# The front of a hybrid decoder block rebuilt: keys projected first, first blocks multiplied chunk by chunk, parts of the preparation moved ahead

## The reference

```python
mod = silu(c) @ w_ada + b_ada
shift1, scale1, gate1, shift2, scale2, gate2 = split(mod, 6)
h = rms_norm(x, norm1_gain) * (1 + scale1) + shift1
proj = h @ w_in
aq, ak, av, dq, dk, dv, dz, dbeta, dalpha, gate_a, gate_b = split(proj)
y_a = sliding_window_attention(rms_norm(aq), rms_norm(ak), av, sinks) @ w_attn_branch
qkv = silu(causal_depthwise_conv([dq, dk, dv]))
g = -exp(dn_a_log) * softplus(dalpha + dn_dt_bias)
od = rms_norm(gated_delta_rule(l2(q), l2(k), v, g, sigmoid(dbeta))) * silu(dz)
y_b = od @ w_dn_branch
mix = (sigmoid(gate_a) * y_a + sigmoid(gate_b) * y_b) @ w_out
x = x + gate1 * mix
h2 = rms_norm(x, norm2_gain) * (1 + scale2) + shift2
x = x + gate2 * peer(h2)      # top-k over 16384 experts, gathers of u and v rows
```

## Time and profile before

| | us |
|---|---|
| median of 3 runs | 2647.77 |
| lowest and highest | 2646.91, 2649.31 |
| the profiled execution, whole | 2649.07 |
| its span, first to last instruction | 2647.2 |
| PE busy in it | 2408.7 |
| DVE busy | 1756.6 |
| ACT busy | 947.5 |
| POOL busy | 734.9 |
| mean granted clock | 0.928 |

### The profile page before, as it was taken

How to read it: one execution, slowest core, us unless ns; L and a number is a source line. 1 busy time by engine, 2 the same in 40 slices (tenths; PEclk the granted TensorE clock), 3 DMA queues, 4 the chain that set the end, 5 groups by cost and what they waited for, 6 DMA issues and landing times.

```text
span 2647.2 us, 34159 instructions
## 1 busy us (share of the span) xinstructions
PE 2408.7 (91%) x13229; PEld 2126.7 (80%) x13229; DVE 1756.6 (66%) x3205; ACT 947.5 (36%) x1628; POOL 734.9 (28%) x661
## 2 busy tenths in 40 slices
PE   8687997878878899988899999989999999999998
PEld 7676776878778778766798999988888888888887
DVE  3468884523425275333398899977888888888887
ACT  1232886020110253222355555543333333333332
POOL 0498500010100000000066653353333333333330
PEclk7798997868869799998999999999999999999999
DMA  6353310000000122321233336689998989899984
GB/s 224 116 155 96 112 49 1 1 1 1 0 0 32 64 87 88 110 98 51 97 124 121 132 128 210 204 306 343 324 318 311 321 314 323 309 328 339 327 312 149
DMA packets 214692, 438.41 MB, mean 166 GB/s; under 512 B 22119, under 2 KB 129808, under 8 KB 214288
## 3 DMA queue, kind: packets, MB, share of 16 engines
q1 hardware_dynamic: 168832, 270.71, 30.4%
q0 software_dynamic: 45568, 163.60, 17.2%
q10 hardware_dynamic: 144, 2.10, 0.2%
HBM read 392.32 MB, written 44.04 MB: 165 GB/s over the span
## 4 chain that ended last, share of the span: by engine, by line
PE 41%; DVE 7%; ACT 1%; issue 1%; DMA 0%; POOL 0%; ACTq 0%; DVEq 0%; POOLq 0%
PE bank L1747 20%; PE bank L1645 5%; DVE hot_j L1963 5%; PE bank L1733 3%; PE bank L1731 3%; PE bank L1732 3%; PE bank L1651 2%; PE bank L1615 2%; DVE hot_i L1958 2%; PE bank L1625 1%; ACT ha L1795 1%; PE bank L1667 1%; DMA vg<-in_peer_v_dram,gidx 0%; DVE o_nat L2027 0%; DVE o_nat L2026 0%
## 5 line engine op out<-in xcount | busy, mean ns | idle before, releaser
L1577 POOL TENSOR_TENSOR ua_lo<-ua,ua_hi 128x512 fp32r<-128x512 f32 x128 | 201.6, 1581 | 576.8 <-ACT ua L1782 576.4
L1747 PE MATMUL bank<-vt_hi,wg_hi 128*128 128x512 f32 x768 | 248.6, 405 | 4.9 <-DVE wg_lo L2017 4.6
L1747 PE MATMUL bank<-vt_lo,wg_hi 128*128 128x512 f32 x768 | 239.1, 393 | 0.0
L1747 PE MATMUL bank<-vt_hi,wg_lo 128*128 128x512 f32 x768 | 238.6, 392 | 0.0
L1570 POOL DMA_INDIRECT ug<-in_peer_u_dram,gidx x128 | 145.6, 1137 | 329.9 <-DVE ug L1973 326.9
L1999 DVE TENSOR_TENSOR vt_lo<-vt_raw,vt_hi 128x1024 fp32r<-128x1024 f32 x128 | 156.2, 1220 | 92.5 <-ACT vt_hi L1869 92.4
L1599 POOL DMA_INDIRECT vg<-in_peer_v_dram,gidx x128 | 131.3, 1026 | 238.2 <-DVE g_acc L1988 226.5
L1645 PE MATMUL bank<-h_hi,ua_hi 128*128 128x384 f32 x512 | 184.2, 360 | 12.3 <-ACT ha L1795 12.0
L1731 PE MATMUL bank<-h_hi,uT_hi 128*128 128x384 f32 x512 | 176.7, 345 | 0.0
L1645 PE MATMUL bank<-h_lo,ua_hi 128*128 128x384 f32 x512 | 174.2, 340 | 0.0
L347 DVE TENSOR_TENSOR mx_lo<-mx_raw,mx_hi 128x2048 fp32r<-128x2048 f32 x32 | 73.2, 2292 | 148.5 <-ACT mx_hi L343 148.5
(11 more groups left out here) (395 smaller groups left out, 5967.9 us busy)
## 6 DMA issues: line engine op xcount, KB each, us to landing
u_raw<-in_peer_u_dram SPq DMA_DIRECT2D x128, 512.0 KB
vt_raw<-in_peer_v_dram SPq DMA_DIRECT2D x128, 512.0 KB
gates<-g_stage SPq DMA_DIRECT2D x12, 2048.0 KB, 8.7
gate<-gates SPq DMA_DIRECT2D x32, 768.0 KB
pj_raw<-in_w_in_dram SPq DMA_DIRECT2D x16, 1024.0 KB, 5.3
ada_w<-in_w_ada_dram POOLq DMA_DIRECT2D x32, 512.0 KB, 4.5
mx_raw<-in_w_in_dram SPq DMA_DIRECT2D x12, 1024.0 KB, 5.2
hid_keep<-ha POOLq DMA_DIRECT2D x64, 192.0 KB, 2.1
```

What stands on the lines that cost most here:

```text
L1577: nc.gpsimd.tensor_tensor(ua_lo[b % 2][:, 4 * q:4 * q + 4, :], ua[b % 2][:, 4 * q:4 * q + 4, :], ua_hi[b % 2][:, 4 * q:4 * q + 4, :].bitca ...
L1747: ins = pe.matmul(y_bank[t][q][:], w[n % 2][:, tok], v[n % 2][:, 512 * q:512 * q + 512], start=(first and i == 0), stop=(last and i == 2))
```

## The change

The condition phase has four buffers for `w_ada`. SP issues slab 0 ahead of x, then the key weights, then slab 2; ACT issues slabs 1 and 3. PE sums slab 0 ahead of x's transposes and the others behind the sums of squares, all in one bank, and DVE adds the bias once. The first two slabs of the projection are now the keys; they are loaded and split within the condition phase, and PE multiplies the first three blocks (`FIRST`) there, a chunk at a time as DVE finishes it. The projection phase starts at block 3. In it `amplitude` comes first on DVE, the key norms' squares behind block 7, the values' low half ahead of the norms' divisions, `decays` ahead of the first convolution. 13 of the 32 sums over `w_ada` stand behind blocks and 19 in the attention steps; POOL fills the masks after chunk 8. The transpose of the running decays moves into the second `mixed`. In the mixing phase slabs 20 and 21, and 24 and 25, are multiplied chunk by chunk in pairs, the second slab three chunks behind (`LAG`), and six of eight mixed chunks are split ahead of slab 21's split.

```diff
-            sp.dma_start(x_nat[:], a["x"].rearrange("o (t p) d -> p (o t) d", p=P)).then_inc(s_x, 16)
...
-            for j in range(ADA_SLABS):
-                if j >= 2:
-                    sp.wait_ge(s_ada, j - 1)
-                sp.dma_start(wada[j % 2][:], wada_v[:, :, 512 * j:512 * j + 512]).then_inc(s_wada[j % 2], 16)
-            sp.wait_ge(s_xt, KC)
+            sp.dma_start(wada[0][:], wada_v[:, :, 0:512]).then_inc(s_wada[0], 16)
+            sp.dma_start(x_nat[:], a["x"].rearrange("o (t p) d -> p (o t) d", p=P)).then_inc(s_x, 16)
             for u in range(2):
-                st.load(sp, 0, u, True, [(slice(0, SLAB), w_in[:, :, SLAB * u:SLAB * u + SLAB])])
+                st.load(sp, 0, u, True, key_pieces(w_in, u))
+            sp.dma_start(wada[2][:], wada_v[:, :, 1024:1536]).then_inc(s_wada[2], 16)
+            for u in range(2):
+                st.load(sp, 1, u, False, [(slice(0, SLAB), w_in[:, :, SLAB * u:SLAB * u + SLAB])])
...
+            def ada(j):
+                pe.wait_ge(s_wada[j], 16)
+                for c in range(4 * j, 4 * j + 4):
+                    for k in range(KC):
+                        last = pe.matmul(bank[7][:, c:c + 1], wada[j][:, k, P * (c % 4):P * (c % 4) + P],
+                                         m.silu_c[:, k:k + 1], start=(k == 0), stop=(k == KC - 1))
+                last.then_inc(s_adac, 1)
+            pe.wait_ge(s_sc, 1)
+            ada(0)
...
-            pe.wait_ge(s_sc, 1)
-            for j in range(ADA_SLABS):
-                pe.wait_ge(s_wada[j % 2], 16 * (j // 2 + 1))
-                if j >= 2:
-                    pe.wait_ge(s_modc, j - 1)
...
-                last.then_inc(s_ada, 1)
+            for j in range(1, ADA_SLABS):
+                ada(j)
+            pe.wait_ge(st.lo_done, 2)
+            for k in range(KC):
+                pe.wait_ge(s_split, k + 1)
+                for i in range(FIRST):
+                    cols = slice(P * (i % 2), P * (i % 2) + P)
+                    pe.matmul(bank[i][:], st.hi[i // 2][:, k, cols], m.h_hi[:, k, :], start=(k == 0), stop=False)
+                    pe.matmul(bank[i][:], st.hi[i // 2][:, k, cols], m.h_lo[:, k, :], start=False, stop=False)
+                    last = pe.matmul(bank[i][:], st.lo[i // 2][:, k, cols], m.h_hi[:, k, :], start=False, stop=(k == KC - 1))
+                    if k == KC - 1:
+                        last.then_inc(st.ready, 1)
...
+            act.wait_ge(s_small, 16 * N_SMALL)
+            for j in (1, 3):
+                act.dma_start(wada[j][:], wada_v[:, :, 512 * j:512 * j + 512]).then_inc(s_wada[j], 16)
...
-            act.wait_ge(s_modc, ADA_SLABS + 1)
+            for u in range(2):
+                st.split_hi(act, u, u, 64, True)
+            act.wait_ge(s_modc, 1)
...
-            for j in range(ADA_SLABS):
...
-            dve.wait_ge(s_modc, ADA_SLABS)
+            for u in range(2):
+                st.split_lo(dve, u, u)
+            dve.wait_ge(s_adac, ADA_SLABS)
+            own(dve, c, nc.vector.tensor_tensor(m.mod[:, 0:16], bank[7][:, 0:16], m.colA[:, 24:40], ALU.add))
...
+                    nc.vector.engine_nop().then_inc(s_split, 1)
+
+
+def key_pieces(w_in, u):
...
+    def multiply_chunks(self, pe, slabs, x_hi, x_lo, done):
+        for s in slabs:
+            pe.wait_ge(self.lo_done, s + 1)
+        pe.wait_ge(self.read, 2 * slabs[0])
+        for k in range(KC + LAG):
+            for s, kk in zip(slabs, (k, k - LAG)):
+                if kk not in range(KC):
+                    continue
+                if s == slabs[0]:
+                    pe.wait_ge(done, kk + 1)
+                u = s % 2
+                for half in range(SLAB_BLOCKS):
+                    b, cols = SLAB_BLOCKS * u + half, slice(P * half, P * half + P)
+                    pe.matmul(self.m.bank[b][:], self.hi[u][:, kk, cols], x_hi[:, kk, :], start=(kk == 0), stop=False)
+                    pe.matmul(self.m.bank[b][:], self.hi[u][:, kk, cols], x_lo[:, kk, :], start=False, stop=False)
+                    last = pe.matmul(self.m.bank[b][:], self.lo[u][:, kk, cols], x_hi[:, kk, :], start=False,
+                                     stop=(kk == KC - 1))
+                    if kk == KC - 1:
+                        last.then_inc(self.ready, 1)
 
...
-    ada_after = {c + 2: [c] for c in range(10)}
-    ada_after.update({12 + t: [10 + 2 * t, 11 + 2 * t] for t in range(NT)})
-    ada_after.update({16 + c - 18: [c] for c in range(18, 23)})
+    ada_after = {i: [c] for c, i in enumerate((6, 8, 9, 10, 11, 12, 14, 15, 16, 17, 18, 19, 20))}
+    ADA_MIXED = len(ada_after)
+    ada_mixed = {i: [] for i in range(STEPS)}
+    for n in range(ADA - ADA_MIXED):
+        ada_mixed[n * STEPS // (ADA - ADA_MIXED)].append(ADA_MIXED + n)
...
-                if i == 18:
+                if i == 8:
...
+                if index(s, half) < FIRST:
...
+                    return
                 u, i, cols = s % 2, index(s, half), slice(P * half, P * half + P)
-                if half == 0:
-                    pe.wait_ge(st.lo_done, s + 1)
+                pe.wait_ge(st.lo_done, s + 1)
...
-                if 23 + i < ADA:
-                    ada(23 + i)
+                for chunk in ada_mixed[i]:
+                    ada(chunk)
...
+                if s == 3:
+                    for n in range(NKV):
+                        squares(n)
             pe.wait_ge(z["vsplit"], 2)
             for t in range(NT):
                 values(t)
                 if t < 2:
-                    for n in range(6 * t, 6 * t + 6):
+                    for n in range(NKV + 4 * t, NKV + 4 * t + 4):
...
-            split(0)
-            split(1)
             for s in range(DN):
                 for half in range(2):
                     copy_out(2 * s + half)
                 split(s + 2)
-                if s == AK - 1:
+                if s == 2:
+                    square(0)
+                    square(1)
+                if s == 3:
                     act.wait_ge(z["vload"], 32)
                     nc.scalar.activation(v_hi[:], v_raw[:], ACT.Copy).then_inc(z["vsplit"], 1)
-            square(0)
-            square(1)
+                    square(2)
+                    square(3)
+                if s == 4:
+                    for n in range(NKV):
+                        act.wait_ge(z["krs"], n + 1)
+                        nc.scalar.activation(krs[:, n, :], krs[:, n, :], ACT.Sqrt).then_inc(z["ksqrt"], 1)
+            square(4)
+            square(5)
             values(0)
-            for n in range(2, 8):
+            for n in range(6, 10):
                 square(n)
             values(1)
-            for n in range(NKV):
-                act.wait_ge(z["krs"], n + 1)
-                nc.scalar.activation(krs[:, n, :], krs[:, n, :], ACT.Sqrt).then_inc(z["ksqrt"], 1)
-            for n in range(8, 12):
-                square(n)
+            square(10)
+            square(11)
             values(2)
...
-            for s in range(DN):
+            amplitude()
+            for s in range(2, 5):
                 st.split_lo(dve, s % 2, s)
-            amplitude()
-            dve.wait_ge(z["vsplit"], 1)
-            v.tensor_tensor(v_lo[:], v_raw[:], v_hi[:].bitcast(F32), ALU.subtract).then_inc(z["vsplit"], 1)
-            st.split_lo(dve, 0, DN)
-            st.split_lo(dve, 1, DN + 1)
             for n in range(NKV):
                 dve.wait_ge(z["ms"], n + 1)
                 v.tensor_scalar(krs[:, n, :], bank[3 + n][:], 1.0 / HD, EPS, ALU.mult, ALU.add).then_inc(z["krs"], 1)
+            dve.wait_ge(z["vsplit"], 1)
+            v.tensor_tensor(v_lo[:], v_raw[:], v_hi[:].bitcast(F32), ALU.subtract).then_inc(z["vsplit"], 1)
+            st.split_lo(dve, 1, 5)
             for n in range(NKV):
                 dve.wait_ge(z["ksqrt"], n + 1)
                 own(dve, c, v.reciprocal(krs[:, n, :], krs[:, n, :]))
                 own(dve, c, v.scalar_tensor_tensor(kn[:, n, P:], kn[:, n, P:], kgain[:, 0:1], krs[:, n, :], ALU.mult, ALU.mult))
+            st.split_lo(dve, 0, DN)
+            st.split_lo(dve, 1, DN + 1)
...
             rates()
+            decays()
             for b in range(SLOTS + 2):
                 if b < BLOCKS:
                     conv(b)
-                if b == 0:
-                    decays()
...
-            pe.wait_ge(z["mlo"], 8)
-            for s in range(OUT, WQ):
+            st.multiply_chunks(pe, (OUT, OUT + 1), mix_hi, mix_lo, z["mlo"])
+            for s in range(OUT + 2, WQ):
...
-            pe.wait_ge(z["split2"], 8)
-            for s in range(WQ, N):
+            st.multiply_chunks(pe, (WQ, WQ + 1), h2_hi, h2_lo, z["split2"])
+            for s in range(WQ + 2, N):
...
+                if s == OUT - 1:
+                    for k in range(KC - 2):
+                        high_mix(k)
                 split(s + 2)
...
-            for k in range(KC):
-                act.wait_ge(z["mixed"], KC + k + 1)
```

(14 more changed lines are left out.)

85 lines of the change are left out of this document (42 added, 43 removed).

## The result

The changed kernel took 2614.75 us (median of 4 runs, 2612.4 to 2615.93) against 2648.54 (2646.91 to 2653.85): a ratio of 0.9868, with a 95% interval of 0.9851 to 0.9885. The forecast was 2611, its range 2592 to 2627. The profiled execution spans 2612.9 us, before 2647.2: 34.3 us less.

What follows compares the result with a forecast made beforehand. PE was taken as the bound, with 73.1 us of its waits targeted. A lead of 22.2 plus 14.7 in mixing gave 36.9 us, so 2612.2 profiled, 2610.9 on the median's scale, forecast 2611, range 2592 to 2627.

Steps and rivals of the forecast that it cites:

- Start: Condition phase: PE's chain starts when slab 0 lands, at 16.2 with shared DMA, a loss of 2.9 us; 13.2 alone.
- First blocks: Condition phase: three blocks multiplied as chunks finish, so block 3 starts at 102.0 instead of 117.4, gain 15.4 us.
- Block 4: Projection: amplitude delays slab 2's low part, PE waits 6.8 us; lead 8.8, less 2.4 for the lower clock, 6.4.
- Key squares: Behind block 7: PE stands 3.4 us for a square, 2.4 for the clock, 3.8 for moved sums; lead -3.2.
- Values: Projection, blocks 12 to 15: the low half is ready early, block 15 ends at 200.0 instead of 213.3, lead 13.3 us.
- Decays: Behind block 15: decays take 17.5 us beside POOL, done at 217.5; PE stands about 6 us.
- First step: First attention step: its numbers come 18.1 us behind the decays, at 235.6 instead of 259.0; lead 22.2 after 1.2 charged.
- Slots: Attention slots: both engines go in step as before, carrying ten more POOL sums, so the lead of 22.2 us stays.
- the rival in which POOL is slow: POOL sets the phase's end, sums handed over two at a time; 2672 us at 12 us per chunk; chance 0.02.
- Mixing: Mixing phase: slab 20 starts 3.1 us earlier, slab 24 11.9 earlier, cost 0.3; together a gain of 14.7 us.
- own signs of being wrong: Block 15 not ending before 208, PE's waits in the slots over 25 us in all, or slab 2 of `w_ada` late.
- DVE is the new bound of the first half: Rival: amplitude meets POOL throughout (24.2 instead of 13.0), the lead loses 11.2 us, time 2622; chance 0.16.

Runs made afterwards that it cites:

- experiment 12: Changed kernel with early amplitude, squares first, POOL waiting out decays, single chunks, slabs 1 and 3 issued after slab 0 lands, silu ahead of that wait: 2587.89 us.
- Experiments 2 to 4: Changed kernel with, in turn, FIRST = 0 (2614.71 us), amplitude moved to the condition phase (2604.84 us), and both edits (2616.69 us).
- experiment 5: Changed kernel with POOL leaving out the product and first two halving additions from chunk 13 on: 2602.77 us.
- experiments 1, 2, 8 and 10: Changed kernel with, in turn: whole slabs in mixing, 2628.42 us; FIRST = 0, 2614.71; POOL waiting out decays, 2609.03; slabs 1 and 3 issued after slab 0 lands, 2610.93.
- Experiment 1: Changed kernel with mixing and second projection waiting for all eight chunks, then multiplying slab by slab: 2628.42 us.

## Why the prediction was right, and where it wasn't

*Start.* Predicted 16.2 for the first sum by half rates, 13.2 alone; measured 15.37, and 12.88 alone (experiment 12). The transfer takes 10.2 us shared and 7.7 to 7.8 alone. So the sharing is shown. The half rates aren't: ACT issued its two slabs from 5.94 on, not at 7.5, and half rates from then would by the same working land slab 0 near 17 (an estimate: 0.9 us alone at 409 GB/s, the other 1.7 MB at half of it). It landed at 15.3, so it kept more than half.

*First blocks.* Product at 84.55 (near 84), block 3 at 104.84 (near 105, in the sum 102.0 + 2.9). Here the sum was right and its reading wrong: it booked "Gain 15.4" to the blocks and then took the waits off again as a separate part. Experiments 2 to 4 show that most of the gain and the wait at block 4 are one: without the early blocks the wait isn't there either.

*Block 4.* Wait 5.2, predicted 6.8. POOL's first product came 7.3 us into the phase (111.44), not 6.6, so the small operations were nearly done: most ran at 0.17 us, three took 0.3 to 0.5, and only the last took 1.81 beside the product; slab 2's low part took 2.3. Block 4 started 11.6 us into the phase, predicted 13.0. The clock behind the wait was charged with 2.4; at 0.51 for 5.35 us it cost 2.6.

*Key squares.* Wait 3.2 (3.4). Charged 2.4 for the clock; the 4.9 us behind the wait show

```profile
145.37:150.30 4.93, 4.93 (x12) 0.71 0.00 0
```

a clock of 0.71, so it cost 1.4. This term comes and goes: behind the same wait of 3.2 us the clock was 0.50 in experiment 5 and 1.00 in experiments 1, 2, 8 and 10. Block 11 ended at 171.4, not 174.1: 1.4 less by block 4's start, 1.2 by this term.

*Values.* Block 15 ended at 198.2 (200.0), 15.1 ahead. *Decays.* Done at 218.7 (217.5), which is 20.5 behind block 15 where I had 17.5; PE stood 9.1 for 6. *First step.* 17.3 behind the decays (18.1), at 236.05 (235.6); lead 23.0 (22.2).

*Slots.* This is the step that failed: "From here on both engines go in step as before: the slots carry ten more POOL sums". I counted PE's side of the ten chunks, 0.28 us each, and not POOL's own operations, which moved from the projection into slots where DVE is on the path. It cost 6.6 us, and the rows for it were there: 31 operations that took 20.06 us beside POOL, 6.4 by their free size. The handover of two at a time, which I named for the rival in which POOL is slow, was the place; it cost by POOL's meeting DVE, not by making PE wait for POOL.

*Mixing.* Waits 4.4 and 7.7 (4.4 and 7.6), gain 16.05 (14.7). Experiment 1 gives 13.8 to the order; I had 3.1 + 11.9 - 0.3. Of the remaining 2.2, 1.9 are the first wait, 5.6 instead of 7.5 with whole slabs, which no run here takes apart.

In all: 0.8 more than predicted up to the first step, 6.6 less by the slots, 1.3 more in the mixing, 1.9 elsewhere; 34.3 for 36.9. That the total came out within 4 us of the forecast is partly luck: the step that failed cost 6.6, and 4.0 of small gains stand against it, of which the 1.9 elsewhere lie in stretches where runs differ by as much. One of the prediction's own signs of being wrong did show: PE's waits in the slots are 12.7 + 9.1 + 3.0 + 1.2 = 26.0 us, over the 25 it had set. "DVE is the new bound of the first half" had a chance of 0.16 as a rival and is half true: not by 11.2 us, but it is why the chunks gave so little by themselves.

## What to carry to other kernels

When work is moved from one place to another, count it on every engine that it runs on, and ask beside what it will run there: POOL's sums were nearly free by PE's account and cost 6.6 us by way of DVE. A gain that ends in a new wait isn't a gain and a cost but one bound that has moved; take away what stands on the engine now waited for (here 31 small operations with nothing to do with it) and the two edits are worth 12 us, where one alone was worth nothing and the other 2.4 to 4.8. And before a queue is made to wait for something, look at what else stands behind that wait. Last, hold a small gain against a run whose edit comes later: here such a run had a lead 2.8 us larger, and two experiments seemed to gain as much.
